# An expert loop in blocks of 32 slots over four column groups, with its sums kept apart from the residual

## The reference

```
h2 = rmsnorm(x, ln_ffn_g) * (1.0 + sc2) + sh2
logits = h2 @ router_w + router_b              # 32 experts
top_v, top_i = lax.top_k(logits, 4); gates = softmax(top_v)
# for each expert e and the rows that chose it:
hdn = x_rows @ w1[e] + b1[e]                   # 1024 -> 2048, g and up
g = min(g, 7); act = (clip(up, -7, 7) + 1) * (g * sigmoid(g * 1.702))
y_rows = act @ w2[e] + b2[e]                   # 1024 -> 1024
f[row] += gate * y_row                         # four experts per row
x = x + g2 * f
```

## Time and profile before

| | us |
|---|---|
| median of 3 runs | 1538.03 (1538.01 to 1538.17) |
| the profiled execution's own time | 1538.22 |
| its span, first to last instruction | 1536.4 |
| PE busy | 1459.3 (95%) |
| DVE busy | 660.2 (43%) |
| ACT busy | 338.7 (22%) |
| POOL busy | 135.0 (9%) |

### The profile page before, as it was taken

One profiled execution on the slowest core, in us unless ns is written; L12 is line 12 of the kernel. 1 busy time (PEld: TensorE's weight loads), 2 busy tenths in 40 slices (PEclk: granted clock), 3 DMA queues, 4 the chain that ended last, 5 costly groups with the idle time before them and its releaser, 6 DMA issues.

```text
span 1536.4 us, 21087 instructions
## 1 busy us (share of the span) xinstructions
PE 1459.3 (95%) x8212; PEld 615.6 (40%) x8213; DVE 660.2 (43%) x1004; ACT 338.7 (22%) x610; POOL 135.0 (9%) x127
## 2 busy tenths in 40 slices
PE   5989899999999969999999999999999999999996
PEld 3456455455555543333333333333333333333332
DVE  1232123663257483443534434434435344354444
ACT  2124332212223241121121211211211212112121
POOL 0000000313238530000000000000000000000000
PEclk9999999999999969999999999999999999999999
DMA  9754542461334959999999999999885999999994
GB/s 375 232 230 157 198 166 89 143 184 62 124 99 158 320 231 411 427 427 429 429 427 428 429 430 429 427 429 429 374 357 233 428 430 428 428 427 430 429 428 195
DMA packets 40606, 495.74 MB, mean 323 GB/s; under 512 B 5461, under 2 KB 6005, under 8 KB 11765
## 3 DMA queue, kind: packets, MB, share of 16 engines
q1 hardware_dynamic: 35700, 480.18, 75.6%
q0 software_dynamic: 4864, 14.98, 3.4%
HBM read 490.41 MB, written 4.73 MB: 322 GB/s over the span
## 4 chain that ended last, share of the span: by engine, by line
PE 85%; DMA 9%; DVE 3%; ACT 2%; issue 1%; POOL 1%; SPq 0%; DVEq 0%; ACTq 0%
PE ps L1952 27%; PE ps L1503 18%; PE ps L1977 15%; DMA memory<-in_w_moe 7%; PE ps L1506 5%; PE ps L1898 5%; PE ps L1883 4%; PE ps L1465 4%; DMA memory<-in_w_dense 2%; PE ps L1481 1%; PE ps L1959 1%; PE ps L1614 1%; PE ps L1641 1%; PE ps L1942 1%; POOL memory L571 1%
## 5 line engine op out<-in xcount | busy, mean ns | idle before, releaser
L1952 PE MATMUL ps<-memory,arena 128*64 128x512 f32 x2176 | 483.3, 596 | 16.0 <-DMA memory<-in_w_moe 8.3
L1503 PE MATMUL ps<-memory,xT 128*128 128x512 f32 x672 | 303.5, 607 | 5.3 <-DMA memory<-in_w_dense 3.4
L1952 PEld LDWEIGHTS ps<-memory,arena 128*64 128x64 f32 x2176 | 152.5, 137 | 307.2 <-issue 285.7
L1977 PE MATMUL ps<-memory,arena 128*64 128x512 f32 x1088 | 248.5, 598 | 0.1
L1503 PEld LDWEIGHTS ps<-memory,xT 128*128 128x128 f32 x672 | 127.4, 194 | 158.3 <-issue 151.6
L1977 PEld LDWEIGHTS ps<-memory,arena 128*64 128x64 f32 x1088 | 72.7, 136 | 146.1 <-issue 138.9
L1441 DVE TENSOR_TENSOR R<-R,xT 128x1024 f32<-128x1024 f32 (+1 forms) x102 | 124.7, 1222 | 3.5
L1430 DVE TENSOR_SCALAR arena<-ps 128x512 f32<-128x512 f32 x34 | 23.5, 692 | 232.1 <-PE ps L1959 232.1
L1438 DVE SCALAR_TENSOR_TENSOR xT<-ps,arena,mod 128x1024 f32<-128x1024 f32 x68 | 87.1, 1281 | 8.8 <-PE ps L1898 8.8
L1898 PE MATMUL ps<-xT,arena 64*128 64x512 bf16 x630 | 85.9, 379 | 2.9 <-DVE xT L1447 2.9
L883 ACT ACTIVATE xT<-ps 128x512 f32<-128x512 f32 x35 | 21.0, 599 | 306.2 <-PE ps L1883 302.0
(11 more groups left out here) (305 smaller groups left out, 1180.1 us busy)
## 6 DMA issues: line engine op xcount, KB each, us to landing
memory<-in_w_moe SPq DMA_DIRECT2D x192, 2048.0 KB, 21.7
memory<-in_w_dense SPq DMA_DIRECT2D x33, 2048.0 KB, 9.1
memory<-in_state POOLq DMA_DIRECT2D x8, 256.0 KB, 7.7
out_sample_retention<-memory POOLq DMA_DIRECT2D x8, 256.0 KB, 5.1
memory<-mod_rows SPq DMA_DIRECT2D x4, 512.0 KB, 9.8
arena<-in_b POOLq DMA_DIRECT2D x9, 128.0 KB, 2.7
R<-in_x_prompt SPq DMA_DIRECT2D x1, 1024.0 KB, 10.4
arena<-in_cache_kT POOLq DMA_DIRECT2D x8, 128.0 KB, 4.4
```

The source lines that it names most:

```text
L1503: last = mm(banks[t][0], xT[:, k, t * P:t * P + P], wv[:, k, :], start=(k == 0), stop=(k == KD - 1), skip_group_check=True)
L1952: last = mm(ps[64 * a:64 * a + 64, half, :], xgT[:, k, j % 2, :], wv[:, k, HALF * a:HALF * a + HALF], start=(j % 2 == 0 and k == 0), stop= ...
L1977: last = mm(ps[64 * a:64 * a + 64, 2, :], actT[:, k, j - 4, :], wv[:, k, HALF * a:HALF * a + HALF], start=False, stop=(j == 5 and k == 3), ...
```

## The change

The blocks have 32 slots, and the output row is cut into four quarters of 256 columns, which land on partitions 0 to 31, 32 to 63, 64 to 95 and 96 to 127 of half a bank. All tiles of a block on DVE and ACT are 256 columns wide instead of 512. On PE the second scatter moves behind unit 4 and the third behind unit 5, the gather is cut in two by the turn of the activations, and b2 is put in ahead of unit 4 (bank 2 first holds the turned activations; bank 0 holds g, then the gathered and turned rows). The scatter uses banks 4 to 7.

DVE adds gate times scattered tile to an array `sums` of its own with one instruction per tile; the multiplication by g2 and the addition to R come once, in the last block, which is written out behind DVE's loop (gate_sums, add_gated). The rows of g2 are loaded behind the last weight unit into ring slot 0. The splitting of h moves from GpSimd to DVE, the clearing of y_parts to ACT; normalise(2), pick_slots, pick_expert(0) and the block counts are reordered at the entry, and fold_gain("s") moves ahead of residual(1, 0).

The core of the diff (SP's waits for the ring are unchanged; in it the new addresses, and what only shortens a row from HALF to QUARTER, are left out):

```diff
-BLOCK = 64
-MAX_BLOCKS = 64
+BLOCK = 32
+MAX_BLOCKS = 72
+QUARTERS = 4
+QUARTER = D // QUARTERS
...
+    sums = [after_router[:, D:2 * D], after_mod[:, 0:D], T[:, 2, :]]
+    last_gates = ring[:, 0, :].rearrange("p (n d) -> p n d", n=4)
+    gate2 = [last_gates[:, 0, :], last_gates[:, 0, :], last_gates[:, 1, :]]
...
 sync
-        load_rows(gate2[0], 10, gate2_in)
...
         load_second_expert(1)
-        load_rows(gate2[2][0:64], 10, gate2_in)
...
+        sp.wait_ge(unit_used, EXPERT_UNITS * blocks + EXPERT_UNITS - 1)
+        load_rows(gate2[0], 10, gate2_in)
+        load_rows(gate2[2][0:64], 10, gate2_in)
         for t in range(2):
             sp.wait_ge(final_ready, t + 1)
...
 gpsimd
-        nc.gpsimd.memset(y_parts, 0.0).then_inc(y_clean, 1)
-        for t in range(3):
-            h_rest_of(t)
-        for t in range(3):
-            h_low_of(t)
...
 scalar
         A(top_gate, top_gate, ACT.Exp).then_inc(top_exp, 1)
+        act.wait_ge(added, 1)
+        act.wait_ge(first_picked, 1)
+        A(y_parts.rearrange("p n c -> p (n c)"), gate_last[:, 0:1].to_broadcast([P, 3 * QUARTER]), ACT.Copy).then_inc(y_clean, 1)
...
             A(g_act, g_cut, ACT.Gelu_apprx_sigmoid).then_inc(g_act_ready, 1)
             take_gathered(i + 1)
             act.wait_ge(actT_done, i)
...
+            take_turned(i + 1)
             act.wait_ge(pickT_done, i)
             act.wait_ge(scattered, 3 * i)
             take_pickT()
-            take_turned(i + 1)
...
 vector, entry
         X.tensor_tensor(pick_first, ...).then_inc(first_picked, 1)
+        normalise(2)
+        pick_slots()
+        pick_expert(0)
...
-        done(X.tensor_scalar(n_of, counted, float(BLOCK), 1.0, ALU.is_gt, ALU.add))
-        for m in range(2, TOKENS // BLOCK):
-            done(X.scalar_tensor_tensor(out=n_of, in0=counted, scalar=float(BLOCK * m), in1=n_of, op0=ALU.is_gt, op1=ALU.add))
+        done(X.tensor_tensor(over, counted.unsqueeze(2).to_broadcast(per_block), iota[:, 1:TOKENS // BLOCK].unsqueeze(1).to_broadcast(per_block), ALU.is_gt))
+        done(X.tensor_reduce(n_of, over, AX.X, ALU.add))
+        done(X.tensor_scalar(n_of, n_of, 1.0, None, ALU.add))
...
+        for t in range(3):
+            h_rest_of(t)
+        for t in range(3):
+            h_low_of(t)
+        for t in range(3):
+            done(X.memset(sums[t], 0.0))
...
 vector, loop
+        def add_block(t, n):
+            r = ROWS[t]
+            dve.wait_ge(scattered, 3 * n + t + 1)
+            X.scalar_tensor_tensor(out=quarters(sums[t][0:r]), in0=ps[0:r, SUM_BANKS:, 0:QUARTER], scalar=gate_last[0:r, t:t + 1],
+                                   in1=quarters(sums[t][0:r]), op0=ALU.mult, op1=ALU.add).then_inc(added, 1)
+        def gate_sums():
+            dve.wait_ge(gate2_in, 16 * (1 + BATCH_S))
+            for t, r in enumerate(ROWS):
+                X.tensor_tensor(sums[t][0:r], sums[t][0:r], gate2[t][0:r], ALU.mult).then_inc(summed, 1)
+            for t, r in enumerate(ROWS):
+                dve.wait_ge(summed, t + 1)
+                X.tensor_tensor(R[0:r, t, :], R[0:r, t, :], sums[t][0:r], ALU.add).then_inc(summed, 1)
+            dve.wait_ge(summed, 6)
...
             X.tensor_scalar(g_cut, ps[:, 0, 0:QUARTER], LIMIT, None, ALU.min).then_inc(g_cut_ready, 1)
+            if last:
+                gate_sums()
             dve.wait_ge(unit_used, EXPERT_UNITS * i + 3)
...
-            for t, r in enumerate(ROWS):
-                dve.wait_ge(scattered, 3 * i + t - 2)
-                X.scalar_tensor_tensor(out=halves(grown[0:r]), in0=ps[0:r, 6:8, :], scalar=gate_last[0:r, t:t + 1], in1=halves(gate2[t][0:r]),
-                                       op0=ALU.mult, op1=ALU.mult).then_inc(added, 1)
-                dve.wait_ge(added, 3 * i + t - 1)
-                X.tensor_tensor(R[0:r, t, :], R[0:r, t, :], grown[0:r], ALU.add).then_inc(summed, 1)
+            for t in range(3):
+                if last:
+                    dve.wait_ge(scattered, 3 * done_blocks + t + 1)
+                    add_gated(t, SUM_BANKS, added, 3 * done_blocks + t + 2, summed, 7 + t)
+                else:
+                    add_block(t, done_blocks)
+                if t == 1:
+                    dve.wait_ge(unit_used, EXPERT_UNITS * i + 4)
+                    pick_expert(e_next)
...
 tensor
             for t, r in enumerate(ROWS):
+                pe.wait_ge(h_ready, t + 1)
+                for q in range(QUARTERS):
+                    last = mm(ps[BLOCK * q:BLOCK * q + BLOCK, 0, 0:QUARTER], pick_first[0:r, t, :], T[0:r, t, QUARTER * q:QUARTER * (q + 1)], ...)
...
+                for q in range(QUARTERS):
+                    rows = slice(BLOCK * q, BLOCK * q + BLOCK)
+                    last = mm(ps[0:r, first + q, 0:QUARTER], pickT[rows, t * P:t * P + r], y_parts[rows, n, :], start=(n == 0), stop=(n == 2))
...
                     for k in range(4):
-                        for a in range(2):
-                            last = mm(ps[64 * a:64 * a + 64, half, :], xgT[:, k, j % 2, :], wv[:, k, HALF * a:HALF * a + HALF], ...)
+                        for q in range(QUARTERS):
+                            last = mm(ps[BLOCK * q:BLOCK * q + BLOCK, half, 0:QUARTER], xgT[:, k % 2, 2 * (j % 2) + k // 2, :], wv[:, k, QUARTER * q:QUARTER * (q + 1)], ...)
...
             scatter(i, 0)
-            gather(i + 1)
+            pe.wait_ge(picked, i + 1)
+            pe.wait_ge(h_split, 3)
+            pe.wait_ge(g_cut_ready, i)
+            gather(0)
+            gather(1)
             pe.wait_ge(act_ready, i)
-            for k in range(4):
-                last = tr(ps[:, 4, k * P:(k + 1) * P], h_act[:, k * P:(k + 1) * P], P)
+            for m in range(2):
+                last = tr(ps[:, 2, m * P:(m + 1) * P], h_act[:, m * P:(m + 1) * P], P)
             last.then_inc(actT_done, 1)
-            scatter(i, 1)
+            gather(2).then_inc(gathered, 1)
             pe.wait_ge(actT_ready, i)
+            add_b2()
             for j in (4, 5):
...
                 if j == 4:
                     turn(i + 1)
-                    scatter(i, 2)
+                scatter(i, j - 3)
```

More of the change, by code:

```diff
@@ L244, in build @@
     rtmp = cut(544, 3, NEXP)
-    slot_base = cut(640, MAX_BLOCKS)
+    slot_base = cut(928, MAX_BLOCKS)
+    over = cut(1024, NEXP, TOKENS // BLOCK - 1)
     of_block = cut(704, 2)
@@ L253, in build @@
     pick_first = cut(832, 3, BLOCK)
-    xgT = cut(1536, 4, 2, BLOCK)
-    actT = cut(2048, 4, 2, BLOCK)
+    xgT = cut(1536, 2, QUARTERS, BLOCK)
+    actT = cut(2048, 2, QUARTERS, BLOCK)
     b2_parts = cut(2560, HALF).bitcast(BF16)
     pickT = cut(3072, 3 * HALF // 8).bitcast(BF16)
[L258 to L262, removed]
+    pick = cut(3264, 3 * HALF // 8).bitcast(BF16).rearrange("p (t q s) -> p t q s", t=3, q=QUARTERS)
+    g_cut = cut(3456, QUARTER)
+    g_act = cut(3968, QUARTER)
+    u_cut = cut(4480, QUARTER)
+    h_act = cut(4992, QUARTER)
     pick_e = cut(5504, BLOCK // 2).bitcast(BF16)
@@ L1873, in gather_first, with gather @@
             last.then_inc(gathered, 1)
-        def gather(n):
-            pe.wait_ge(picked, n)
-            pe.wait_ge(h_split, 3)
-            for t, r in enumerate(ROWS):
-                parts = [(part, r) for part in h_parts[t]] if t < 2 else [(packed, P), (h_parts[t][2], r)]
-                for m, (part, rows) in enumerate(parts):
-                    for a in range(2):
-                        last = mm(ps[64 * a:64 * a + 64, 3, :], pick[0:rows, t, 0, :], part[0:rows, HALF * a:HALF * a + HALF],
-                                  start=(t == 0 and m == 0), stop=(t == 2 and m == 1), skip_group_check=True)
-            last.then_inc(gathered, 1)
+        def gather(t):
+            r = ROWS[t]
+            parts = [(part, r) for part in h_parts[t]] if t < 2 else [(packed, P), (h_parts[t][2], r)]
+            for m, (part, rows) in enumerate(parts):
+                for q in range(QUARTERS):
+                    last = mm(ps[BLOCK * q:BLOCK * q + BLOCK, 0, 0:QUARTER], pick[0:rows, t, 0, :], part[0:rows, QUARTER * q:QUARTER * (q + 1)],
+                              start=(t == 0 and m == 0), stop=(t == 2 and m == 1), skip_group_check=True)
+            return last
@@ L1887, in turn @@
         def turn(n):
             pe.wait_ge(xg_rows, n)
-            for c in range(4):
-                last = tr(ps[:, 3, c * P:(c + 1) * P], xg_s[:, c * P:(c + 1) * P], P)
+            for c in range(2):
+                last = tr(ps[:, 0, c * P:(c + 1) * P], xg_s[:, c * P:(c + 1) * P], P)
             last.then_inc(turned, 1)
         def scatter_tile(t, first):
+            r = ROWS[t]
             for n in range(3):
-                for a in range(2):
-                    last = mm(ps[:, first + a, :], pickT[64 * a:64 * a + 64, t * P:(t + 1) * P], y_parts[64 * a:64 * a + 64, n, :],
-                              start=(n == 0), stop=(n == 2))
+                for q in range(QUARTERS):
+                    rows = slice(BLOCK * q, BLOCK * q + BLOCK)
```

(2 more changed lines are left out.)

150 lines of the change are left out of this document (74 added, 76 removed).

## The result

The changed kernel takes 1691.85 us (median of 4 runs, 1689.14 to 1695.81) against 1538.06: 1.1002 times the time before, 95% interval 1.0988 to 1.1016. Forecast were 1594 us and a range up to 1635. The direction was right, the size was not: 98 us are missing. The profiled execution took 1689.14 us, its span is 1687.3, and the mean granted PE clock 0.944 (0.977 before).

A forecast was written before the change was run, and what follows sets the result against it. PE was taken as the bound, with weight transfers nearly full: 588.8 through block 1, 57x16.0 for blocks, 60 for waits, 17 less 0.6 for the last block, 15.5 for the end: span 1592.7, forecast 1594 us; likeliest 1570 to 1625, wider 1545 to 1635.

The forecast's parts named there:

- the entry: Work ahead of the expert loop: reordered, it lets the loop start at 564.6 and block 1 end at 588.8 us, before 603.3.
- what PE waits for in a block: Two waits of PE on ScalarE copies, 0.92 and 0.6 us, added to 14.4 us of work: a block of 16.0 us.
- 58 of them are 928 us: Sum over the expert loop: 58 blocks of 16.0 us take 928 us, so PE saves only 6.
- PE's own work: PE's matmuls and transposes in one block of 32 slots, without waits: 14.4 us, of which 10.75 for the weight units.
- The handovers: Two PE waits in each block, no longer covered: 0.92 us for the activations' copy, 0.6 us for the picks' copy.
- The ring: Eight-slot weight queue in the expert loop: PE waits 56 us in 28 waits around one-block experts, none over 3.1.
- restarts: PE starting again after waits for weights in the expert loop: an estimated 0.15 us each, 4 us in all.
- The last block: Last block of the expert loop waits for late gate rows: 15 us, and 2 for a clock that fell meanwhile.
- Rival B: Both PE waits on ScalarE copies in a block are hidden: block 14.4 us, total 1549 us; chance 0.11.
- C: Only three of four column groups run side by side: 71 ns a record, 2.9 us more a block, 1695 us; chance 0.07.
- D: Weight transfers set the end, with blocks under 14.4 us and gate rows not holding the last block: 1528 us; chance 0.08.
- E: PE's clock falls in waits for weights: six starved stretches each pay 3 us more, 1612 us; chance 0.08.

## Why the prediction was wrong

The bill, against the prediction's own sum (span 1592.7, measured 1687.3): block 1 ended at 583.2 instead of 588.8, -5.6 (all of it in the entry: the block began at 558.9 instead of 564.6; over the other kernels with this entry it began between 559.5 and 564.4, so part of it may be the run's own variation); the seven turns, +82; 56 blocks at 16.54 instead of 16.0, +30; five blocks that starve for weights, 48 us over usual ones, instead of 60, -12; last block and end, 47.7 instead of 47.9, 0 (by luck: 30.7 and 17.0 us against 32.4 and 15.5). That makes +94, and 94.6 are missing.

- **The failed step** is "what PE waits for in a block" together with its sum "58 of them are 928 us". It took PE to stand only on other engines and transfers, and gave no price to its own instruction supply, though the change nearly doubles PE's instructions in a block (twice as many matmuls, each half as long). That term is 82 us, 5.8 to 6.4 us of each turn on the jump's own record, shown from both sides: it goes without the jump, and it comes into the kernel before with a longer body.
- **PE's own work** was taken at 14.4 us; with everything else removed it is 14.95 (0.03 us of it idle). Four groups side by side were right (10.64 us for the units, forecast 10.75). The scatters (0.45 each), gathers (1.24 in all) and turns (0.74) are each a little over their terms.
- **The handovers**: copy of the activations 0.73 us, taken away by exchanging two ScalarE lines (forecast 0.92); copy of the picks 0.55 in second blocks (forecast 0.6). Rival B is out: both waits are real.
- **New experts**: 0.5 us more wherever an expert begins, from the read of two bounds, of which the copy of the picks covers the rest. No step had it; 31x0.5 = 16 us of the 30 above. The kernel before reads the same bounds under its last unit of 3.6 us; moving the third scatter behind that unit, which the prediction priced by the copy alone, bared them too.
- **The ring**: 48 us in the experts after one-block experts, 56 and 4 forecast (no row shows the 4 for restarts). The split was wrong: some 33 us are waits, the longest 3.0 (forecast 3.1), and some 15 are matmuls at the lower clock. One of the forecast's places (expert 8) lay in the shadow of a turn's stall; without the stalls the waits were 40.5, with blocks of 14.95 us 65.9.
- **The last block**: gate rows at 1653.0, the hole 12.5 us and the half clock behind it, forecast 15 and 2.
- **Rivals.** C gave 1695, close to what came, but by a mechanism that is not there: a record takes 54 to 56 ns, not 71. (The 3.07 that it quotes from the Trainium skill, TensorE: Matmul & The Clock Gate, Measured speedup vs the span model, is there a figure for four matmuls packed over rows; these four, packed over columns, reach 95 to 99% of four, 53.3 against 54 to 56 ns.) D is out: even without the waits a block takes 14.95 us, not under 14.4. E was right in its mechanism: the clock fell in all five starved blocks, not only behind the stalls on instructions, and cost some 3 us in each, E's own price. One such stretch, with no turn in it (PE's busy time first, its clock ahead of the last two):

```profile
745.00:755.00 10.00, 7.94 (x92) 3.37 (x96) 1.03 (x3) 0.00 (x0) 0.00 (x0) 0.54 1.00 424
```

E's 1612 was still far off, for want of the same term as 1594.

## What to carry to other kernels

When a change makes instructions smaller and more numerous, count the instructions of the loop body, not only their time: here the jump back over up to 1368 matmuls and weight loads took 0.22 us. From 1624 on it took some 6 us and cost 9 to 13 us in the changed kernel and its shortened forms, most of it idle and the rest at the lower clock, and 7 to 9 us where a whole unit was still queued behind it. At all seven jumps of the changed kernel the DMA engines were full with weights (share 1.00 to 1.03); what a jump costs beside idle ones no run shows. The profile's signs are a wait on "issue" at the same place in every turn, a long branch record at the loop's line, and instruction packets that go on after the first turn; writing the loop out removes them. And when one wait is covered, look at what else starts at the same time under it: here a 1.1 us wait that the profile put down to ScalarE's copy ended 0.65 us after that copy. It was a read of registers, and went only when it was read a block ahead.

## What the runs showed of the hardware that was not expected

- The refetch at a jump back: 5.8 to 6.4 us on the branch, 7.2 to 7.9 us idle and 11.7 us in all per turn for 2232 matmuls and weight loads; 0.22 us on the branch at 1368; inner loops that jump back over one block (558) took at most 0.25.
- Reading two loop bounds on PE between two loops: 1.0 us idle where only a scatter of 0.5 us is queued ahead of it; no idle time in the kernel before, where a whole unit of 3.6 us is.
- Straight-line code of 32 experts ran without a stall on instructions beyond the entry's 3.5 us, at 97 instruction packets.
